# A two-layer decoder trunk on one core: two kept weight chunks per layer, a ring of ten slots, split chunk loads, and phase ends copied out by halves

## The reference

```python
def block(xb):                       # 128 tokens
    q = einsum('nd,de->ne', xb, w_q).reshape(n, PEER_HEADS, 2, PEER_HALF)
    s = einsum('nhie,ike->nhik', q, keys)
    top_s, top_i = lax.top_k(s, PEER_TOPK)
    ...
    best_s, best_pos = lax.top_k(cand_s, PEER_TOPK)
    idx = jnp.take_along_axis(cand_i, best_pos, axis=-1)
    gate = jax.nn.softmax(best_s, axis=-1)
    u = expert_u[idx]
    act = jax.nn.gelu(jnp.einsum('nhkd,nd->nhk', u, xb))
    coef = gate * act
    return jnp.einsum('nhk,nhkd->nd', coef, expert_v[idx])
```

## Time and profile before

| | |
|---|---|
| median of 3 runs | 1629.3 us (1629.07 to 1630.72) |
| the profiled execution | 1629.12 us |
| its span, from first to last instruction | 1627.3 us |
| moved by DMA in it | 665.05 MB, mean 409 GB/s |
| busy: PE, DVE, ACT, POOL | 1202.7, 1171.0, 527.0, 600.7 us |

### The profile page before, as it was taken

One profiled execution on the slowest core, in us unless ns is written; L12 is line 12 of the kernel. 1 busy time (PEld: TensorE's weight loads), 2 busy tenths in 40 slices (PEclk: granted clock), 3 DMA queues, 4 the chain that ended last, 5 costly groups with the idle time before them and its releaser, 6 DMA issues.

```text
span 1627.3 us, 21833 instructions
## 1 busy us (share of the span) xinstructions
PE 1202.7 (74%) x7488; PEld 591.0 (36%) x7488; DVE 1171.0 (72%) x3339; ACT 527.0 (32%) x1231; POOL 600.7 (37%) x542
## 2 busy tenths in 40 slices
PE   8876786868748887978687788799697855555565
PEld 3661232225415663533264355444234611111111
DVE  4479768668768687786677866788956886666665
ACT  0222143222224564642132355455311232222221
POOL 1034433533334244233333323441433345444442
PEclk9998897989879998998898799999798988777767
DMA  9879999999999999999999999999999989999997
GB/s 380 339 297 412 423 421 421 422 421 421 421 417 415 423 425 420 420 423 422 422 422 422 384 424 424 421 421 417 395 414 424 416 354 421 422 421 421 421 421 315
DMA packets 84079, 665.05 MB, mean 409 GB/s; under 512 B 9376, under 2 KB 9392, under 8 KB 11008
## 3 DMA queue, kind: packets, MB, share of 16 engines
q0 software_dynamic: 74752, 540.13, 80.3%
q1 hardware_dynamic: 9216, 123.53, 18.0%
HBM read 662.57 MB, written 1.05 MB: 408 GB/s over the span
## 4 chain that ended last, share of the span: by engine, by line
DMA 29%; PE 29%; DVE 26%; ACT 7%; issue 7%; POOL 2%; another core or an unknown queue 0%; DVEq 0%; POOLq 0%; ACTq 0%; SPq 0%
DMA ring<-in_experts,idx 28%; PE acc L928 11%; DVE ring L1584 9%; PE act_bank L610 7%; PE dve_bank L596 6%; DVE h L1390 2%; DVE onehot L1219 2%; DVE scratch L1219 2%; POOL ring L500 2%; ACT diag L1148 1%; ACT L990 1%; ACT h L1070 1%; PE act_bank L596 1%; ACT scratch L990 1%; PE act_bank L890 1%
## 5 line engine op out<-in xcount | busy, mean ns | idle before, releaser
L500 POOL DMA_INDIRECT ring<-in_experts,idx x510 | 573.5, 1125 | 947.6 <-PE acc L928 732.0
L928 PE MATMUL acc<-ring,diag 64*64 64x512 f32 x4080 | 608.2, 720 | 315.8 <-ACT diag L1148 307.9
L1584 DVE CUSTOM_DVE_ANT_0 ring<-ring,hn 128x1024 f32<-128x1024 f32 x512 | 620.7, 1224 | 220.1 <-DMA ring<-in_experts,idx 197.1
L928 PEld LDWEIGHTS acc<-ring,diag 64*64 64x64 f32 x4080 | 155.1, 153 | 665.2 <-ACT diag L1148 427.2
L1141 ACT ACTIVATE acts<-dots 128x2 f32<-128x2 f32 x256 | 52.1, 203 | 674.6 <-DVE dots L1584 642.2
L610 PE MATMUL act_bank<-hnT,wbuf 128*128 128x128 f32 x1728 | 218.0, 284 | 23.3 <-ACT h L1070 19.5
L1148 ACT ACTIVATE diag<-cst,coefs 128x64 f32<-128x64 f32 x512 | 150.3, 340 | 252.1 <-DVE coefs L1592 215.4
L610 PEld LDWEIGHTS act_bank<-hnT,wbuf 128*128 128x128 f32 x1728 | 205.2, 197 | 70.1 <-issue 63.0
L990 ACT ACT_TABLE_LOAD x80 | 102.6, 1283 | 19.4 <-DMA rowc<-in_rows 17.0
L1592 DVE TENSOR_TENSOR coefs<-acts,gate 128x2 f32<-128x2 f32 x256 | 42.7, 167 | 79.5 <-ACT acts L1141 64.7
L1141 ACT ACT_TABLE_LOAD x68 | 87.2, 1283 | 6.2 <-DVE dots L1584 0.3
(11 more groups left out here) (173 smaller groups left out, 1024.8 us busy)
## 6 DMA issues: line engine op xcount, KB each, us to landing
wbuf<-in_weights SPq DMA_DIRECT2D x48, 2048.0 KB
ring<-in_weights SPq DMA_DIRECT2D x7, 2048.0 KB, 19.4
ring<-in_experts,idx POOLq DMA_INDIRECT x510
kept<-in_weights SPq DMA_DIRECT2D x2, 2048.0 KB, 21.8
wbuf<-in_weights SPq DMA_DIRECT2D x2, 1024.0 KB, 7.0
scratch<-in_bias POOLq DMA_DIRECT2D x1, 1024.0 KB, 12.0
scratch<-in_bands POOLq DMA_DIRECT2D x1, 768.0 KB, 13.3
h<-in_x SPq DMA_DIRECT2D x1, 512.0 KB, 3.7
```

The source lines that it names most:

```text
L500: pool.indirect_dma_start(ring[:, n % RING], None, io[f"experts{layer}"], bass.IndirectOffsetOnAxis(idx[:, at:at + 1], 0),).then_inc(sem(f ...
L928: last[rows] = pe.matmul(acc[rows][half][home:home + HALF_P], diag[part, n % DIAGS], ring[part, slot, D + half * CW:D + (half + 1) * CW], ...
L1584: dve.tensor_tensor_reduce(out=ring[:, slot, 0:D], in0=ring[:, slot, 0:D], in1=hn[:, phase % NBLK], scale=1.0, scalar=0.0, op0=ALU.mult, o ...
```

## The change

1. `KEPT` names two chunks a layer instead of one: 58 loads of 2 MB become 56, and the kept buffer doubles. The ring gives the room: `RING` goes from 12 to 10, and six chunks are staged instead of seven.
2. Loads into `wbuf` whose number is in `PARTED = range(12, LOADED, 7)` are issued as two DMAs, of 120 and of 8 partitions. PE waits for the sum of both (`chunk_landed`). `LOADED` comes to 46, so there are five of them, 12, 19, 26, 33 and 40.
3. The end of a phase: ACT signals after each half of its copies, DVE copies the even sums out by halves (`copy_even`), without waiting for ACT, and adds the odd ones one slot later (`add_odd`). PE sums the first half of the new phase's first pair as soon as that half was copied by both. `take_stream` goes to n = 7, behind three pairs, and adds to what is there.
4. At the start ACT handles two heads before the first softmax part (`ROUTED_HEADS = 2`) and DVE two before the first dot product (`TOPS_FIRST = 2`, `TOPS_DUE` is new); PE makes the gain rows ahead of head 0. The later parts of head 1's choice of experts are due from slot 4 of a phase on (`ROUTE_FROM`).

```diff
-RING = 12
+RING = 10
...
-STAGED_AT = (5, 3, 0, 1, 2, 4, 5)
+STAGED_AT = (4, 3, 0, 1, 2, 4)
...
-KEPT = ((7,), (13,))
+KEPT = ((7, 9), (13, 15))
...
+LOADED = sum(kind == "wbuf" for kind, _ in HOMES)
+PARTED = range(12, LOADED, 7)
+WIDE = 120
+
+
+def chunk_landed(n):
+
+    return 16 * (n // NWB + 1 + sum(m <= n and m % NWB == n % NWB for m in PARTED))
...
-EARLY_HEADS, ROUTED_HEADS = 6, 3
+EARLY_HEADS, ROUTED_HEADS = 6, 2
...
+TAKEN_AT = 3 * GROUP + 1
...
+ROUTE_FROM = 4
...
+            if _head == 1:
+                _due = max(_due, _phase * SLOTS + ROUTE_FROM + _part - 1) if _phase and _part else max(_due, _part)
+            ROUTE_DUE.append(_due)
...
-TOPS_FIRST = 3
-TOPS_DUE = [-3, -2, -2, 0, 1, 1, 3, 5]
+TOPS_FIRST = 2
+TOPS_DUE = [-3, -2, 0, 1, 2, 3, 4, 5]
...
-                            sp.dma_start(wbuf[:, n % NWB].rearrange("p k c -> p (k c)"), w
-                                         ).then_inc(sem(f"chunk_in{n % NWB}"), 16)
+                            into = wbuf[:, n % NWB].rearrange("p k c -> p (k c)")
+                            if n in PARTED:
+                                sp.dma_start(into[0:WIDE], w[0:WIDE]).then_inc(sem(f"chunk_in{n % NWB}"), 16)
+                                sp.dma_start(into[WIDE:P], w[WIDE:P]).then_inc(sem(f"chunk_in{n % NWB}"), 16)
+                            else:
+                                sp.dma_start(into, w).then_inc(sem(f"chunk_in{n % NWB}"), 16)
...
             def take_stream(phase):
...
-                                        start=True, stop=False, skip_group_check=True)
+                                        start=False, stop=False, skip_group_check=True)
...
             def sum_pair(g, q, start=False, stop=False):
...
                 for half in range(2):
+                    if start and g:
+                        pe.wait_ge(sem("even_copied"), 2 * (g // STEPS - 1) + half + 1)
+                        pe.wait_ge(sem("odd_copied"), 2 * (g // STEPS - 1) + half + 1)
...
-                                                   start=start and odd == 1, stop=stop, skip_group_check=True)
+                                                   start=start, stop=stop, skip_group_check=True)
...
             def experts(phase, beside):
...
-                    if n == GROUP:
-                        if phase:
-                            pe.wait_ge(sem("acc_read"), phase)
-                            pe.wait_ge(sem("odd_copied"), phase)
-                        take_stream(phase)
...
+                    if n == TAKEN_AT:
+                        take_stream(phase)
...
             def copy_odd(phase):
...
-                lane.after(started)
-                lane.tell("odd_copied")
+                    lane.after(started)
+                    lane.tell("odd_copied")
...
-            def read_acc(phase):
+            def copy_even(phase):
...
-                        started = lane.start(dve.tensor_tensor(h[part, phase % NBLK, cols], odd_sums[part, cols],
-                                                               acc[rows][half][part], ALU.add))
-                lane.after(started)
-                lane.tell("acc_read")
+                        started = lane.start(dve.tensor_copy(h[part, phase % NBLK, cols], acc[rows][half][part]))
+                    lane.after(started)
+                    lane.tell("even_copied")
+
+            def add_odd(phase):
+
+                for half in range(2):
+                    lane.need("odd_copied")
+                tt(h[:, phase % NBLK], h[:, phase % NBLK], odd_sums, ALU.add)
...
                     if n == GROUP and phase:
-                        read_acc(phase - 1)
+                        copy_even(phase - 1)
+                    if n == GROUP + 1 and phase:
+                        add_odd(phase - 1)
```

More of the change, by code:

```diff
@@ L145 @@
                 _due = _phase * SLOTS - 15.5 + 1.5 * _part
-            ROUTE_DUE.append(max(_due, _part) if _head else _due)
-TOPS_FIRST = 3
-TOPS_DUE = [-3, -2, -2, 0, 1, 1, 3, 5]
+            if _head == 1:
[3 more added lines that the diff above has]
+TOPS_DUE = [-3, -2, 0, 1, 2, 3, 4, 5]
 for _phase in range(1, PHASES):
@@ L579, in next_chunk @@
                     return staged[:, at].rearrange("p (k c) -> p k c", k=KD)
-                pe.wait_ge(sem(f"chunk_in{n % NWB}"), 16 * (n // NWB + 1))
+                pe.wait_ge(sem(f"chunk_in{n % NWB}"), chunk_landed(n))
                 return wbuf[:, n % NWB]
@@ L870, in queries @@
                     transposes(h[:, b, half * CW:(half + 1) * CW], 4)
+                for half in range(2):
+                    out = fill("dve")
+                    for j in range(4):
+                        row = layer * KD + 4 * half + j
+                        ins = pe.matmul(out[:, j * P:(j + 1) * P], ident[:, row:row + 1].to_broadcast([P, P]),
+                                        gain_rows, start=True, stop=True)
+                    ins.then_inc(sem("dve_full"), 1)
                 for hd in range(PH):
@@ L892, in queries @@
                     ins.then_inc(sem("act_full"), 1)
-                    if hd == 0:
-                        yield at + 3
-                        for half in range(2):
-                            out = fill("dve")
-                            for j in range(4):
-                                row = layer * KD + 4 * half + j
-                                ins = pe.matmul(out[:, j * P:(j + 1) * P], ident[:, row:row + 1].to_broadcast([P, P]),
-                                                gain_rows, start=True, stop=True)
-                            ins.then_inc(sem("dve_full"), 1)
             def side(layer, b):
@@ L1593, in coefficients @@
                                   ALU.mult).then_inc(sem("coef_done"), 1)
-            def read_acc(phase):
+            def copy_even(phase):
                 for rows in range(2):
                     dve.wait_ge(sem(f"pairs_summed{rows}"), (phase + 1) * STEPS * GROUPS + AHEAD)
-                lane.need("odd_copied")
                 for half in range(2):
```

## The result

| | before | after |
|---|---|---|
| median of four runs | 1630.01 us (1629.07 to 1631.11) | 1674.84 us (1674.29 to 1676.31) |
| the profiled execution's span | 1627.3 us | 1672.2 us |
| moved by DMA, mean rate | 665.05 MB, 409 GB/s | 660.86 MB, 395 GB/s |

The ratio is 1.028, 95% interval 1.026 to 1.029: the change makes the kernel 45 us slower. It moves 4.2 MB less, as it should, and needs more time for it. The forecast of 1613 us and its range missed.

A forecast was written before the change was run, and what follows sets the result against it. It took the kernel as a DMA stream at 422 GB/s with holes of lower rate. Span 1627.3 minus 9.9 (bytes), 2 (start) and 4.7 (interior holes) is 1610.7; with 1.8 outside 1612.5, forecast 1613 us, range 1603 to 1631.

The forecast's parts named there:

- The split loads: Five loads of 120 and 8 rows: 5 us gained in each hole to 3.1 us lost in the whole.
- The last sentence of the prediction: Wrong as a whole if the full DMA rate changed, for instance if split loads ran on few engines; no size.
- The lag of one engine: One DMA engine some 5 us behind; if relieved, gathers land up to 5 us earlier where DVE waits.
- Bytes: Chunk loads: 58 become 56, two times 2.097 MB less, 9.9 us gained at 422 GB/s; bounds 5 and 9.9.
- Ring: Two slots fewer in the gather queues: up to 5.0 us more in each hole where queues are nearly dry.
- the relief: The lagging DMA engine spared rows by the split: landings up to 5 us earlier, cancelling the ring's 5.0.
- ten slots are too few: Rival, chance 0.06: the ring alone acts, five holes of 5.0 us each, phase ends' gain eaten; 1642 us.
- Phase ends: Three phase ends: PE's first sum 6 us earlier each, against holes of 11.6 us together.
- Start: First dot products some 5 us earlier, gathers behind the first sum earlier: 2 us gained; bounds 2 lost, 5 gained.
- The first rival: The split misses the lag, holes follow the ring: 1628 us, between 1622 and 1634; chance 0.32.

The follow-up runs named there:

- kept2_ring10: The kernel before with ten ring slots instead of twelve, two kept chunks a layer and six staged chunks, nothing else changed: 1630.76 us, ratio 1.0036.
- ring10: The kernel before with ten ring slots instead of twelve, one kept chunk a layer, seven staged chunks in five homes: 1648.66 us, ratio 1.0108.
- nosplit: The changed kernel with every chunk load whole again (PARTED empty), all else as changed: 1631.85 us, ratio 1.0011.
- nosplit_b: The changed kernel without split loads, run again in another group beside three other kernels: 1629.57 us, ratio 1.0026.

## Why the prediction was wrong

**The split loads** are the step that failed. The prediction priced them by shares: an engine relieved of 5.0 us each time, others with 0.6 us more, bounds of 5 us gained in each hole and 3.1 us lost in the whole. Measured: 43 to 46 us lost. Both bounds took the time of a row, 0.62 us at 422/16 GB/s, as given, and asked only who gets how many. But that time came from loads of 128 partitions, and the earlier trace rows hold no load of another shape. For a form that the trace does not show it is no bound. The last sentence of the prediction named the case ("if the full rate itself changed"), but gave it neither price nor chance; the reason put there, few engines, is not what happened, since the DMA share stays at 1. A rival with half the rate while a split load runs would have stood at 25 us or more, as an estimate: five loads of 5.0 us each take twice as long, and the gathers beside them stretch this. The runs show 43 to 46 us. The rule of the Trainium skill (DMA: Bandwidth & Descriptors, "Rules for kernel authors") that the prediction weighed made it 1.7 us, and no run agrees with that size.

**The lag of one engine** was the hope behind that step. DVE's waits for gathers were 214.0 us without the split and 262.4 with it, against 197.1 before: nothing was relieved. Whether one engine lags at all no run shows, since the traces have no engine numbers.

**Bytes:** minus 9.9. The 4.2 MB went, but what they gave in time stays open: `kept2_ring10` against `ring10` gives 12 us with an error of nearly 4, and 7.4 us of it are the start's staging.

**Ring:** the mechanism was right (wider holes, two stretches that open, one of them seen at 640 us), the term was not. I let the ring's 5.0 us in each hole cancel against the relief and put 6 us for the rest. There was no relief, so all of it is paid: 11 us by `ring10` without its loss at the start, 15.8 by `kept2_ring10` if the bytes gave their full 9.9. The errors of the two ratios don't settle which. The rival "ten slots are too few" went further, to 1642 us; without the split the kernel takes 1632, so that case did not come about, and its low chance is not contradicted.

**Phase ends:** the earlier first sum is there, 6 us forecast, 4.9, 5.3 and 6.4 measured with twelve slots, and 7.0 in the kernel after at the third. PE's rows there, against the earlier trace rows, where the first pair ended at 1322.90, 14.1 us behind the pair before it (now 1358.55 behind 1351.46):

```profile
1347.82 3.64 PE L947 MATMUL acc<-ring,diag 64*64 64x512 f32 x16 [2.06 <-ACT diag L1164]
1355.12 3.43 PE L947 MATMUL acc<-ring,diag 64*64 64x512 f32 x16 [3.66 <-DVEq L375]
1360.06 1.95 PE L947 MATMUL acc<-ring,diag 64*64 64x512 f32 x16 [1.50 <-ACT diag L1164]
1367.05 3.69 PE L947 MATMUL acc<-ring,diag 64*64 64x512 f32 x16 [5.05 <-ACT diag L1164]
```

What failed is the step from there to the time. The question "what is late next" had an answer in the traces: DVE, with hardly a gap through the phase end, gives the third pair its coefficients so late that it starts 20 us behind the old phase. The forecast let phase ends and relief close 10.7 us of holes and kept 4.7 of it after the ring's 6; the phase ends by themselves give nothing that can be told with twelve slots and 3 to 6 us with ten.

**Start:** minus 2 forecast, with 2 us lost as the bound. Measured 0.14 and 0.25% lost with twelve slots, 0.07 and 0.29% with ten: 1 to 5 us lost, of which the 1 is within the error. I followed the first sum and the gathers that wait for it, and did not follow ACT's wait for DVE behind the moved choice of experts.

Of the sum, then, in us: ring and bytes plus 6 together (1.0036), phase ends minus 3 to 6, start plus 1 to 5, split plus 43. Without the split that is 1631 to 1638, and `nosplit` took 1632 (1634 by the ratio of `nosplit_b`). The first rival, with 1628 and its range of 1622 to 1634, was nearest to this, but by luck: it priced the split at 1 us, with the rate at 422, and its ring and phase ends, 28 us lost and 18 gained, were both too large.

## What to carry to other kernels

Do not cut a load by partitions to balance engines: cut it by columns, or leave it whole. Look at GB/s beside the DMA share: here a share of 1 at half the rate came from the form of a load and not from an empty queue. A price per row or per byte holds for the shapes in the trace alone; a shape that the trace does not have needs a rival in which the rate itself changes. Where a stall of one engine is shortened, look for the engine that has no gap through the stretch: the gain at the first step can be given back two steps on. And when a run isolates one part, look whether it brought a cost of its own: 8 of the 18.7 us of `ring10` came from a staged chunk without a home of its own.

## What the runs showed of the hardware

- A load from HBM into 120 partitions halves what the DMA engines move together while it runs (201 to 224 GB/s against 422): alone it runs at 205 GB/s, and beside it the gathers are slowed too. Each 2 MB load cut so costs 8 to 9 us. 64 and 64 partitions run at 211 GB/s for 13 us, 112 and 16 at 240 GB/s for 12 us, and cost about 6 us each.
- The same chunk as two DMAs of 128 partitions by 8 KB runs at 423 GB/s.
- Source rows 16384 or 16896 bytes apart in HBM make no difference to this (1674.8 us, and 1676.6 us in one run).
- The DMA share can't tell this from a full stream: it was 0.97 to 1.05 at half the rate.
